# Combining the two softmaxes of differential attention on GpSimd in two steps, in place of one VectorE instruction

## The reference, cut to what matters

```
s = einsum('bhcqd,bhckd->bhcqk', q, k) * (A_DQK ** -0.5)      # c: the two halves of a head
p = softmax(s, axis=-1)
w = p[:, :, 0] - lam * p[:, :, 1]
o = einsum('bhqk,bhkd->bhqd', w, v)
...
o = _rms_norm(o.transpose(0, 2, 1, 3), g, eps=1e-5) * (1.0 - lam_init)
```

## Time and profile before

| | us |
|---|---|
| median of 3 runs | 3127.11 (3121.96 to 3128.09) |
| span of the profiled execution | 3122.2 |
| TensorE busy | 2874.1 (92%) |
| VectorE busy | 1948.0 (62%) |
| ScalarE busy | 1237.8 (40%) |
| GpSimd busy | 563.5 (18%) |
| wide combines on VectorE (L2175) | 103.1 in 72 |

### The profile page before, as it was taken

The page is one execution under the profiler, slowest core; times in us unless marked ns, Lnnn a source line. Parts: engine busy times, 40 slices in busy tenths (PEclk is TensorE's granted clock), DMA queues, the critical chain, the costliest instruction groups (busy, mean ns, idle before and its releaser), DMA issues.

```text
span 3122.2 us, 47135 instructions
## 1 busy us (share of the span) xinstructions
PE 2874.1 (92%) x17730; PEld 1614.1 (52%) x17730; DVE 1948.0 (62%) x2706; ACT 1237.8 (40%) x2368; POOL 563.5 (18%) x449
## 2 busy tenths in 40 slices
PE   5999886889889999999999899988889999999997
PEld 3555553554545556757755554554554444444443
DVE  5875786992575404636655687578964673374765
ACT  5212446883543212313334411447863542231332
POOL 0022010001318102202212004010003161121211
PEclk9999997998999999999999799999999999999998
DMA  5211111222143320111131311113322332111143
GB/s 213 75 41 36 36 46 65 93 79 66 57 149 125 118 81 35 51 44 41 55 136 54 141 41 41 45 46 102 120 79 88 129 121 74 48 56 53 54 148 109
DMA packets 69316, 248.95 MB, mean 80 GB/s; under 512 B 9248, under 2 KB 10016, under 8 KB 69152
## 3 DMA queue, kind: packets, MB, share of 16 engines
q1 hardware_dynamic: 68000, 241.44, 22.9%
q10 hardware_dynamic: 1152, 5.24, 0.4%
HBM read 221.75 MB, written 19.92 MB: 77 GB/s over the span
## 4 chain that ended last, share of the span: by engine, by line
PE 63%; issue 19%; DVE 10%; ACT 5%; DMA 1%; POOL 1%; SPq 0%; POOLq 0%; DVEq 0%; ACTq 0%
PE PS L809 38%; PE PS L978 18%; DVE wlo L1938 2%; PE PS L830 2%; DVE R L2117 1%; ACT whi L1431 1%; DVE R L2104 1%; PE PS L1188 1%; ACT SW L1791 1%; DMA R<-in_w_ada 1%; ACT X L1550 1%; ACT R L1548 1%; DVE X L2405 1%; PE PS L1233 1%; PE PS L934 0%
## 5 line engine op out<-in xcount | busy, mean ns | idle before, releaser
L809 PE MATMUL PS<-R,whi 128*128 128x512 f16 (+1 forms) x4992 | 1353.8, 358 | 40.6 <-DVE wlo L1938 24.3
L809 PE MATMUL PS<-R,wlo 128*128 128x512 f16 (+1 forms) x2496 | 893.9, 358 | 0.0
L809 PEld LDWEIGHTS PS<-R,whi 128*128 128x128 f16 x4992 | 486.5, 98 | 540.5 <-issue 38.5
L978 PE MATMUL PS<-R,whi 128*128 128x256 f16 (+2 forms) x2352 | 510.2, 326 | 0.0
L1938 DVE SCALAR_TENSOR_TENSOR wlo<-stage,whi 128x1024 f16<-128x1024 f32 (+1 forms) x204 | 279.2, 1369 | 364.0 <-ACT whi L1431 362.8
L809 PEld LDWEIGHTS PS<-R,wlo 128*128 128x128 f16 x2496 | 245.5, 98 | 240.5 <-issue 7.1
L978 PE MATMUL PS<-R,wlo 128*128 128x256 f16 (+2 forms) x1176 | 319.1, 326 | 0.0
L978 PEld LDWEIGHTS PS<-R,whi 128*128 128x128 f16 x2352 | 230.1, 98 | 151.9
L1431 ACT ACTIVATE whi<-stage 128x1024 f16<-128x1024 f32 (+1 forms) x204 | 210.5, 1032 | 138.1 <-PE PS L809 85.0
L2143 DVE TENSOR_REDUCE tiny<-PS 128x1 f32<-128x1280 f32 (+1 forms) x144 | 197.1, 1369 | 29.9 <-PE PS L1006 29.4
L1967 DVE TENSOR_TENSOR X<-X,PS 128x256 f32<-128x256 f32 (+2 forms) x294 | 151.0, 550 | 96.1 <-PE PS L978 95.9
(11 more groups left out here) (227 smaller groups left out, 3577.4 us busy)
## 6 DMA issues: line engine op xcount, KB each, us to landing
stage<-in_w_gu SPq DMA_DIRECT2D x120, 512.0 KB, 3.8
X<-in_w_ada SPq DMA_DIRECT2D x60, 512.0 KB, 3.3
stage<-in_w_down SPq DMA_DIRECT2D x48, 512.0 KB, 3.5
stage<-in_w_in SPq DMA_DIRECT2D x44, 512.0 KB, 3.3
stage<-in_w_out SPq DMA_DIRECT2D x32, 512.0 KB, 3.2
h_save<-R SPq DMA_DIRECT2D x24, 640.0 KB, 5.3
R<-h_save SPq DMA_DIRECT2D x24, 640.0 KB, 4.9
T<-in_w_ada SPq DMA_DIRECT2D x20, 512.0 KB, 3.6
```

What stands on the lines that cost most here:

```text
L809: last = mm(slot(into, t0, t1)[:, c0 - t0:c1 - t0], w[:, j, k, :], row, start=(k == 0 and q == 0), stop=(k == K - 1 and q == 2))
L978: last = mm(s_bank(nf, t, o, n), w[:, j, k0 + k, :], row, start=(k == 0 and x == 0), stop=(k == PAIRS - 1 and x == 2))
```

## The change

VectorE keeps the ratio, now in two alternating columns of `beta`, and signals it through a new semaphore `ratio`. GpSimd waits for it, multiplies the second exponentials by it in place (TENSOR_SCALAR), waits for its own instruction, and adds the first ones (TENSOR_TENSOR), after which it signals `w`. The wait on `wt_ps` moves to GpSimd with it. Its loop over tiles is now written out, and the root of a tile's mean square comes before the combine of head 2 of the next tile. On VectorE only the last tile's end has a new wait, for its own `rinv`.

```diff
-                    ratio = own.mark(STT(beta[:, 0:1], den[:, h % 2, 0:1], lamv[:, 10 + l:11 + l], rec[:, h, 1:2], ALU.mult, ALU.mult))
+                    STT(beta[:, h % 2:h % 2 + 1], den[:, h % 2, 0:1], lamv[:, 10 + l:11 + l], rec[:, h, 1:2],
+                        ALU.mult, ALU.mult).then_inc(s("ratio"), 1)
                     if h == HA - 1:
-                        own.mark(TS(rinv, rec[:, :, 0], 1.0 / XS, None, ALU.mult))
+                        scaled = own.mark(TS(rinv, rec[:, :, 0], 1.0 / XS, None, ALU.mult))
+                        if isinstance(r, int) and r == nt - 1:
+                            own.reach(scaled)
                     if norm is not None:
                         out_norm(norm)
-                    own.reach(ratio)
-                    if not (isinstance(r, int) and n < 2):
-
-                        dve.wait_ge(s("wt_ps"), NG * n - NG + before("wt_ps"))
-                    STT(Wt[h % 2][:, 0:keys], P2[h % 2][:, 0:keys], beta[:, 0:1], P1[h % 2][:, 0:keys],
-                        ALU.mult, ALU.add).then_inc(s("w"), 1)
...
-                per = 4 + 8 + 1 + 2
+                per = 4 + 4 + 1 + 2
...
-                    done = tiles_before(l, run)
-                    with pool.Fori(0, nt) as r:
-                        pool.wait_ge(S["o_var"], r + (done + 1))
+                    done, NG, keys = tiles_before(l, run), len(key_groups(nk)), nk * P
+                    before = lambda name: heads_before(l, run, name)
+
+                    def combine(n):
+
+                        pool.wait_ge(S["ratio"], n + 1 + before("ratio"))
+                        if n >= 2:
+
+                            pool.wait_ge(S["wt_ps"], NG * n - NG + before("wt_ps"))
+                        own.link(nc.gpsimd.tensor_scalar(P2[n % 2][:, 0:keys], P2[n % 2][:, 0:keys], beta[:, n % 2:n % 2 + 1],
+                                                         None, ALU.mult))
+                        TT(Wt[n % 2][:, 0:keys], P2[n % 2][:, 0:keys], P1[n % 2][:, 0:keys], ALU.add).then_inc(S["w"], 1)
+
+                    def out_root(r):
+
+                        pool.wait_ge(S["o_var"], r + done + 1)
                         TT(st8[:, 2, 0:4], st8[:, 1, 0:4], nhalf[:, 0:1].to_broadcast([P, 4]),
                            ALU.pow).then_inc(S["o_pow"], 1)
+
+                    for n in range(HA * nt):
+                        if n % HA == 2 and n > HA:
+                            out_root(n // HA - 1)
+                        combine(n)
+                    out_root(nt - 1)
```

More of the change, by code:

```diff
@@ L285, in build @@
         ring_landed = [sem(f"ring_landed{j}") for j in range(3)]
-        S |= {n: sem(n) for n in "scores nbias maxed exps w wt_ps wt pv pv_out".split()}
+        S |= {n: sem(n) for n in "scores nbias maxed exps ratio w wt_ps wt pv pv_out".split()}
         X16 = X[:, :].bitcast(F16)
```

## The result

The changed kernel takes **3453.01 us** (median of 4 runs, 3451.68 to 3454.37) against 3124.83 us for the kernel before (4 runs): a ratio of 1.1052, 95% interval 1.1038 to 1.1066. It is 328 us slower, twice the 162 us that the sum gave, and 68 us above the top of the range. The direction, the place and the ring of waits were forecast; the size was not.

The account below looks back on a forecast made before the run. A ring of waits through the combine was taken to bound the kernel. Latent tiles 137, context heads 5 and clock 20 sum to 162 us; with the 3122.2 span and 4.9 offset, 3289 us (5.2% slower), range 3228 to 3385.

Parts of the forecast that it names:

- the ring of waits: Attention, latent heads: combine, transposes, copy, second exponential, reciprocal and ratio wait on each other, 5.33 us per head.
- The combine itself stands on the path that sets the end: Plain latent slot: VectorE's wide combine, 1.55 us, lies on the ring of waits once per head.
- VectorE's other work is beside the ring: Plain latent slot: VectorE's work other than the combine does not lie on the ring of waits.
- The rival "faster": Latent tiles: VectorE is the real bound and the weights are not urgent; 50 us less, 3077; chance 0.03.
- Taking the wide instruction off VectorE gives nothing back: Latent heads: the maxima come earlier, but what waits for them waits for the weights too, so no gain.
- The scale: GpSimd's one-input multiply over 1280 columns: 1.3 us, bounded by 1.2 and the add's 2.9.
- the dear case: Rival on GpSimd: the scale costs as much as the add, 2.9 us; 102 us more, 3391; chance 0.12.
- The clock: TensorE in attention: gaps lower the granted clock half of the time, 0.35 us per head, some 20 us.
- Contention: Slot 3 of a latent tile: VectorE's `out_norm` and GpSimd's scale compete for SBUF, 0.5 us per tile.
- The two engines take turns, one instruction each: VectorE instructions with two SBUF inputs and GpSimd's instructions alternate; seen as 2.37 us in place of 0.69.
- The context heads: The 8 context heads: scale some 0.3, add 0.61 and hand-overs replace a 0.48 combine; about 0.6 each, 5 us.
- low clock throughout: Rival in attention: TensorE's clock stays low, every slot 8.8 us; 43 us on top of 142, 3312; chance 0.12.

Follow-up runs that it names:

- a scale of 1.31 us: The changed kernel with GpSimd's scale over only the first 400 columns, the other 880 left without their factor; 3288.9 us.
- the TENSOR_SCALAR of 2.20 us above: Wide combine shared: VectorE takes columns 0 to 511, GpSimd 512 to 1279 by scaling and adding; the kernel before has all on VectorE; 3149.3 us.

## Why the prediction was wrong

- **"The combine itself stands on the path that sets the end"**: right for a longer combine, and the ring's sum gives the changed kernel's turns to 0.03 us at full clock. "VectorE's other work is beside the ring" was wrong before the change: VectorE was busy for 5.43 us of one turn of 5.46, and splitting the combine lengthened turns by what it cost VectorE. The rival "faster" had that half right. "Taking the wide instruction off VectorE gives nothing back" was right here, for the ring is now far longer than VectorE's work.
- **Hand-overs**, 0.08, 0.08 and 0.13 us: right (0.10, 0.09, 0.14 in the turn shown).
- **The add**, 2.9 us: right, 2.88.
- **The scale**, 1.3 us: this is the step that failed. It was priced as half of a two-input instruction "since nothing but the number of inputs differs", and bounded above by the add, "which does everything the scale does and reads one more row". The runs bear out neither: it measured 3.54, above the add's 2.88. The mis-sized term is 2.24 x 64 = 143 us, of the 164 between forecast and result, and with a scale of 1.31 us the time is 3288.9. The upper bound was what broke the range: the dear case was priced at 3391 with a scale of 2.9, and the range stopped just short of it. One form's duration had been taken for a bound on another form, and no row of GpSimd's TENSOR_SCALAR existed. The estimate that the prediction worked out from the Trainium skill (GPSIMD Engine Reference, section 4.1, Engine selection), which has one-input operations roughly at line rate, was lower still, 1.07 us; the measurement disagrees by a factor of 3.3.
- **The clock**, some 20 us: right in kind, too small. It cost 0.64 us a head, 41 us, where 0.35 were counted, and keeping TensorE busy gave back 39. "Half of the time low" was right, for the granted clock was 0.73 to 0.77 in the windows after, between 0.5 and 1. But the low half was not spread evenly: with the longer scale it fell on the ring's transposes and scores in most turns, behind TensorE's wait. A slow turn cost 0.9 us ("0.6 to 0.8" were counted); at the low clock the ring goes through the scores and the maxima, not through ScalarE. The 24.4 us taken for every tile of the first layer came from one at a clock of 0.93; in the mean it was 23.5, which is 7 us of the miss.
- **Contention**, 0.5 us per tile: nearly absent from the turns. The one in which `out_norm` meets the scale is 10.99 us, no longer than its neighbours, and the scale takes 3.63 in place of 3.52. It is there in single instructions: `out_sum`'s squares (L2180) took 2.26 us at the median against 0.43 before, as forecast hidden behind the add. "The two engines take turns, one instruction each" does not hold for every pair, as the end of this document shows.
- **The context heads**, 0.6 us each: 1.3, for the scale of 256 columns takes 0.96 us in place of some 0.3.
- **The rivals**: low clock throughout (3312) did not happen: TensorE was busy for 27.6 of 44.4 us and the clock went to and fro. The scale as dear as the add was nearest in kind, though still 0.64 us too cheap. All rows of GpSimd's arithmetic had two inputs, so they said nothing of a one-input form either way, and a chance of 0.12 was too small for that.

## What to carry to other kernels

Find how many paths of about the same length bound a loop before pricing an edit. Lengthening the combine was paid in full, while cutting its urgent part gave nothing; and doubling an instruction lengthens both the ring and its engine's own work, so it can't tell these two apart. Where an operation's form has no row in the trace, another form is no upper bound: leave the range open by a factor, or measure the form. Moving work to an idle engine put that engine's longer instructions on the ring here. Even the part that was not urgent did not pay, for it slowed what VectorE did meanwhile.

## What the runs showed of the hardware

- GpSimd's TENSOR_SCALAR over 1280 float32 columns took 3.52 us (3.47 with a constant), against 2.88 for an add of two rows, 2.35 for a product with a broadcast column, and 0.89 for TENSOR_SCALAR on VectorE. From 256 columns (0.92 us at the least, 0.96 in the mean) and 400 (1.31) to 1280 it costs about 2.5 ns a column.
- Whether VectorE waits for a whole GpSimd instruction depends on which one it is. Beside GpSimd's two-input add the squares of `out_sum`, two SBUF inputs, started at 633.74 and ended at 636.00, just after the add (632.84 to 635.72), and the same 0.28 us after it in all 14 such tiles of the changed kernel:

```profile
632.84 2.88 POOL L2729 TENSOR_TENSOR R<-R 128x1280 f32<-128x1280 f32 x1
...
633.74 2.26 DVE L2180 TENSOR_TENSOR R<-R 128x256 f32<-128x256 f32 x1
```

  Beside the TENSOR_SCALAR of 2.20 us above, a VectorE instruction with two SBUF inputs ended 0.75 us before it did: slowed from 0.75 to 1.41 us, not blocked. In the same kernel a TENSOR_TENSOR of VectorE with two SBUF inputs (L2199), begun while the TENSOR_SCALAR ran, took its usual time:

```profile
634.60 2.21 POOL L2738 TENSOR_SCALAR R<-R,tiny 128x768 f32<-128x768 f32 x1 [0.89 <-DVE tiny L2170]
...
635.97 0.41 DVE L2199 TENSOR_TENSOR R<-R,st 128x256 f32<-128x256 f32 x1
```

  The order counts too: in the 8 of 64 heads in which VectorE's 512 columns started first, by 0.07 us, they took 0.75 us, and GpSimd's TENSOR_SCALAR 2.76 in place of 2.20. The rule of the Trainium skill (SBUF — State Buffer, section Who interferes with whom), an exclusive lock for the whole instruction, fits what VectorE did beside the add, and not what it did beside a TENSOR_SCALAR that already ran.
- More work on TensorE made the program faster (3414 against 3453 us), with no other edit: the granted clock was 0.88 in place of 0.76.
